# Dense per-head attention in a streaming two-layer decoder trunk

## The reference, cut to what matters

```
proj  = h @ w_in                       # 2048 query columns, 48 gate columns
q     = rms_norm(proj[:, :2048] per head of 128, q_gain)
gates = sigmoid(proj[:, 2048:])        # 3 branches x 16 heads
for each query block of 128 rows, each head (4 heads share one k, v):
    for branch in (compressed: 15 keys, selected: 256, window: 256):
        s = q . k / sqrt(128) - slope(head) * distance      # causal mask
        o += gate(branch, head) * softmax(s) @ v
out = concat(o) @ w_o
```

## Time and profile before

| | |
|---|---|
| median of 3 runs | 2630.6 us (2624.01 to 2635.27) |
| profiled execution, its own time | 2624.72 us |
| its span, first to last instruction | 2622.9 us |
| PE busy | 2535.5 us, 97% |
| DVE, ACT, POOL busy | 2154.7, 1251.6, 378.1 us |
| last product of `kv` to first of `wo` | about 1522.9 to 1768.6 us |
| first score product | about 1670.7 us |

### The profile page before, as it was taken

How to read it: one execution, slowest core, us unless ns; L and a number is a source line. 1 busy time by engine, 2 the same in 40 slices (tenths; PEclk the granted TensorE clock), 3 DMA queues, 4 the chain that set the end, 5 groups by cost and what they waited for, 6 DMA issues and landing times.

```text
span 2622.9 us, 38552 instructions
## 1 busy us (share of the span) xinstructions
PE 2535.5 (97%) x14006; PEld 2183.9 (83%) x14006; DVE 2154.7 (82%) x2593; ACT 1251.6 (48%) x1654; POOL 378.1 (14%) x205
## 2 busy tenths in 40 slices
PE   6998999998999999999999999999899999999999
PEld 4876888887888888888887888788788888888887
DVE  7887998999999889988899877678989756765665
ACT  4435343544554355535544444573555435543553
POOL 0000110231120012001142300363112001200110
PEclk8999999999999999999999989999999999999999
DMA  9997688886878877787776877208677655555553
GB/s 373 375 355 271 256 335 330 324 328 247 303 281 303 325 274 286 303 337 291 285 257 245 323 266 293 113 1 304 251 281 276 234 180 191 182 186 191 179 176 145
DMA packets 94312, 685.49 MB, mean 261 GB/s; under 512 B 10465, under 2 KB 10465, under 8 KB 11233
## 3 DMA queue, kind: packets, MB, share of 16 engines
q1 hardware_dynamic: 93746, 681.27, 69.4%
q10 hardware_dynamic: 432, 2.38, 0.2%
HBM read 681.51 MB, written 2.10 MB: 261 GB/s over the span
## 4 chain that ended last, share of the span: by engine, by line
PE 79%; DVE 6%; DMA 2%; issue 2%; ACT 1%; POOL 0%; DVEq 0%; ACTq 0%; SPq 0%
PE banks L1487 48%; PE banks L1489 25%; DMA raw<-in_stream 2%; DVE raw L1100 2%; DVE w_lo L1084 2%; PE banks L777 1%; ACT w_hi L921 1%; PE banks L1476 1%; PE banks L741 1%; PE banks L763 1%; DVE scratch L851 1%; PE banks L780 1%; DVE temp L1168 0%; PE banks L1478 0%; PE banks L743 0%
## 5 line engine op out<-in xcount | busy, mean ns | idle before, releaser
L1487 PE MATMUL banks<-h_op,w_hi 128*128 128x512 f32 x3840 | 1359.0, 399 | 25.6 <-DVE h_op L1174 18.2
L1084 DVE TENSOR_TENSOR w_lo<-raw,w_hi 128x1024 fp32r<-128x1024 f32 x841 | 1092.2, 1321 | 338.4 <-ACT w_hi L921 335.5
L921 ACT ACTIVATE w_hi<-raw 128x1024 fp32r<-128x1024 f32 x841 | 875.0, 1055 | 992.5 <-PE banks L1489 570.2
L1489 PE MATMUL banks<-h_op,w_lo 128*128 128x256 f32 x3840 | 1082.9, 282 | 0.0
L1487 PEld LDWEIGHTS banks<-h_op,w_hi 128*128 128x128 f32 x3840 | 726.0, 189 | 203.0 <-issue 23.8
L1487 PE MATMUL banks<-act_op,w_hi 128*128 128x512 f32 x2176 | 764.3, 397 | 0.3 <-DVE w_lo L1084 0.3
L1489 PEld LDWEIGHTS banks<-h_op,w_lo 128*128 128x128 f32 x3840 | 731.8, 191 | 0.0
L1489 PE MATMUL banks<-act_op,w_lo 128*128 128x256 f32 x2176 | 610.8, 281 | 0.0
L1100 DVE CUSTOM_DVE_ANT_0 raw<-raw,c_all 128x2048 f32<-128x2048 f32 x224 | 553.4, 2486 | 17.0 <-ACT c_all L895 9.5
L1487 PEld LDWEIGHTS banks<-act_op,w_hi 128*128 128x128 f32 x2176 | 409.4, 188 | 98.2 <-DVE w_lo L1084 1.2
L1489 PEld LDWEIGHTS banks<-act_op,w_lo 128*128 128x128 f32 x2176 | 412.2, 189 | 0.0
(11 more groups left out here) (158 smaller groups left out, 1369.8 us busy)
## 6 DMA issues: line engine op xcount, KB each, us to landing
raw<-in_stream SPq DMA_DIRECT2D x645, 1024.0 KB, 5.5
x_res<-in_x SPq DMA_DIRECT2D x1, 2048.0 KB, 11.6
out_x<-x_res SPq DMA_DIRECT2D x4, 512.0 KB, 4.4
mix_area<-in_w_s ACTq DMA_DIRECT2D x1, 1024.0 KB, 9.8
mix_area<-in_b_s ACTq DMA_DIRECT2D x1, 1024.0 KB, 14.3
small<-in_small SPq DMA_DIRECT2D x1, 682.0 KB, 16.6
attn_area<-in_pos ACTq DMA_DIRECT2D x1, 273.0 KB, 5.6
c_all<-in_c SPq DMA_DIRECT2D x1, 8.0 KB
```

Source lines behind the costliest of these rows:

```text
L921: act.activation(w_hi[:, out, 0:n], raw[:, slot, half:half + n], ACT.Copy).then_inc(hi_ready, 1)
L1084: dve.tensor_tensor(w_lo[:, out, 0:n], raw[:, slot, half:half + n], w_hi[:, out, 0:n].bitcast(F32), ALU.subtract).then_inc(stream, 2 if ch ...
L1487: pe.matmul(banks[:, g + j, :], hi[:, k, P * j:P * (j + 1)], operand[:, kt, :], start=(kt == 0), stop=False, skip_group_check=True)
L1489: last = pe.matmul(banks[:, g + j, 0:T], lo[:, k, P * j:P * (j + 1)], operand[:, kt, 0:T], start=False, stop=(kt == last_kt), skip_group_c ...
```

## The change

Four things are changed, all in layer 1 ahead of `wo`.

1. The order of the phases is now `kv`, `cmp`, `gate`, `q` (all four chunks). `h_op` is made during `cmp`. The pieces are the same 35; the first query chunk has three modulation pieces and the others two.
2. A query chunk is summed in one bank region: hi by the high tokens, hi by the low tokens, lo by the high tokens, each 256 columns (three products, each with its weight load, in place of two). ACT alone copies it out and squares it.
3. The prologue is cut into hooks that all engines call at fixed subs of the query chunks. Queries are now normed in place: sums of squares by group of four heads, root and inverse, spread over the partitions by PE, one multiplication on DVE. The last group's hooks lie in the attention loop. POOL makes a distance-times-slope table for every head.
4. The attention loop has 16 steps, one for a head with both query blocks. Scores are one product of 256 and one of 512 columns; DVE adds the bias table and takes the minimum in one instruction for each of four parts, from PSUM. The compressed branch is done once for four heads. Transposes go to one set of banks (six for each head), and the value product is done once for a group of four heads, in eight products of 512 columns (`weigh`).

The core of the diff:

```
-            phases.append(("q", [Chunk("q", 0, "F3", ("q", 0))]))
-            phases.append(("cmp", [Chunk("cmp", 0, "P0", ("cmp", 0))]))
-            phases.append(("q1", [Chunk("q", 1 + i, "P3", ("q", 0)) for i in range(3)]))
+            phases.append(("cmp", [Chunk("cmp", 0, "F3", ("cmp", 0))]))
             phases.append(("gate", [Chunk("gate", 0, "G1", ("gate", 0))]))
+            phases.append(("q", [Chunk("q", i, "P2" if i else "P3", ("q", 0)) for i in range(4)]))
...
+PE_HOOKS = {("q", 0, 1): [("keys", None)], ("q", 0, 4): [("cmp_keys", None)], ("q", 0, 6): [("spread_keys", None)],
+            ("q", 1, 2): [("gates", None)]}
+SPLIT_HOOKS = {("q", 0, 4): [("keys", None)], ("q", 0, 7): [("cmp_keys", None)], ("q", 1, 1): [("spread_keys", None)],
+               ("q", 1, 5): [("gates", None)]}
+for g in range(3):
+    PE_HOOKS.setdefault(("q", g + 1, 3), []).append(("sums", g))
+    PE_HOOKS.setdefault(("q", g + 1, 6), []).append(("spread", g))
...
+        def attention_act(act):
+            for i in range(NH + 7):
+                if i < NH:
+                    n, g, r = i, i // GRP, i % GRP
+                    for k, (qb, b, part) in enumerate(parts(n)):
+                        act.wait_ge(scores_biased, 2 * n + qb + 1)
+                        last = act.activation(part, part, ACT.Exp, scale=-1.0, bias=stat(n, NEG, k, 1),
+                                              accum_out=stat(n, DEN, k, 1))
...
+                if 2 <= i < NH + 2:
+                    act.wait_ge(weights_turned, n + 1)
...     (copies turned_low; for r == 0 four copies of turned_cmp)
+                if i >= 6 and (i - 6) % GRP == 0 and (i - 6) // GRP < NKV:
+                    act.wait_ge(pv_done, g + 1)
...     (two copies of 512 columns to act_op, out_hi)
+        def biased(dve, n):
+            dve.wait_ge(qk_done, n + 1)
+            for k, (qb, b, part) in enumerate(parts(n)):
+                last = dve.tensor_tensor_reduce(
+                    part, banks[:, 2 * (n % 2) + qb, keys * b:keys * (b + 1)], table(g, r)[:, T - keys:T], -1.0, 3e38,
+                    ALU.add, ALU.min, stat(n, NEG, k, 1))
...
+        def attention_dve(dve):
+            for i in range(NH + 7):
+                if i < NH:
+                    biased(dve, i)
+                if 1 <= i < NH + 1:
+                    weighted(dve, i - 1)
+                if i == 2:
+                    prologue_dve(dve, "sums", 3)
+                if i == 5:
+                    prologue_dve(dve, "spread", 3)
+                if 2 <= i < NH + 2:
+                    dve.wait_ge(weights_turned, n + 1)
+                    dve.tensor_copy(probs_t[:, 2:6, r, :], turned_high...)
+                if i >= 6 and (i - 6) % GRP == 0 and (i - 6) // GRP < NKV:
...     (two subtractions of 512 columns after out_hi, then out_lo)
+        def build_tables(pool):
+            pool.wait_ge(cmp_done, 1)
+            for g in range(NKV):
+                for r in range(GRP):
+                    last = pool.tensor_scalar(table(g, r), pos, -slopes[GRP * g + r], None, ALU.mult)
...
+        def attention_pe(pe):
+            score(pe, 0)
+            for i in range(NH + 7):
+                if i + 1 < NH:
+                    score(pe, i + 1)
+                if i == 1:
+                    prologue_pe(pe, "sums", 3)
+                if i == 4:
+                    prologue_pe(pe, "spread", 3)
+                if i >= 6 and (i - 6) % GRP == 0 and (i - 6) // GRP < NKV:
+                    weigh(pe, (i - 6) // GRP)
+                if 2 <= i < NH + 2:
+                    pe.wait_ge(weights_scaled, n + 1)
+                    if n:
+                        pe.wait_ge(turned_read, n)
+                        pe.wait_ge(turned_low_read, n)
...     (six transposes, then weights_turned)
...
+                    elif one_sum(cur.first):
+                                pe.matmul(out, hi[:, k, P * j:P * (j + 1)], operand[:, kt, 0:T],
+                                pe.matmul(out, hi[:, k, P * j:P * (j + 1)], operand[:, kt, T:HILO], start=False,
+                                last = pe.matmul(out, lo[:, k, P * j:P * (j + 1)], operand[:, kt, 0:T], start=False,
```

More of the change, by code:

```diff
@@ L513, in group @@
             return 4 * (prev.static(lambda c: c.n["c"] % 2))
[L516 to L526, removed]
@@ new lines, in scores, with parts, stat, out_of @@
+        def scores(n):
+            return attn_area[:, 768 * (n % 4):768 * (n % 4) + 768]
+        def parts(n):
+            sc = scores(n)
+            return [(0, 0, sc[:, 0:128]), (0, 1, sc[:, 128:256]), (1, 0, sc[:, 256:512]), (1, 1, sc[:, 512:768])]
+        def stat(n, kind, i=0, m=4):
+            o = 6688 + 16 * kind + 4 * (n % 4) + i
+            return attn_area[:, o:o + m]
+        NEG, DEN, COF = 0, 1, 2
+        def out_of(qb):
+            return banks[:, 6 + qb, :].rearrange("p (r t) -> p r t", r=GRP)
@@ new lines, in prologue_act @@
+        def prologue_act(act, what, g):
+            if what == "sums":
+                act.wait_ge(q_sums, g + 1)
+                act.activation(r_q, banks[0:GRP, 6, 0:T], ACT.Sqrt, scale=1.0 / HD, bias=eps[0:GRP, :]) \
+                    .then_inc(q_roots, 1)
+            if what == "keys":
+                act.wait_ge(vcmp_zeroed, 1)
+                act.wait_ge(cmp_done, 1)
+                for r in range(GRP):
+                    last = act.activation(vcmp[32 * r:32 * r + NCMP, :], banks[32 * r:32 * r + NCMP, 6, :], ACT.Copy)
+                act.activation(sq_c, banks[:, 5, 0:NB], ACT.Square).then_inc(cmp_keys_squared, 1)
+                act.wait_ge(square_sums, 1)
+                act.activation(r_k, banks[0:16, 7, 0:T], ACT.Sqrt, scale=1.0 / HD, bias=eps[0:16, :])                     .then_inc(rms_taken, 1)
+            if what == "cmp_keys":
+                act.wait_ge(square_sums, 2)
+                act.activation(r_c, banks[:, 5, 0:NB], ACT.Sqrt, scale=1.0 / HD, bias=eps[:, :]).then_inc(rms_taken, 1)
+            if what == "spread_keys":
+                act.wait_ge(zsum, BY_NAME["gate"][0].n["zsum"] + 1)
+                act.activation(gates_t, gates_t, ACT.Sigmoid).then_inc(gates_ready, 1)
@@ L1034, in evacuate @@
                     act.activation(vstat[:, 18:20], vstat[:, 20:22], ACT.Sqrt).then_inc(vrstd, 1)
-                if e == 3 and first and name == "wo":
+                if e == 0 and first and name == "wo":
+                    prologue_act(act, "sums", 3)
                     attention_act(act)
@@ L1051, in step @@
                                 evacuate_v(*what)
+                        for what in SPLIT_HOOKS.get((name, cur.first.loc, u), []) if name in ("q", "wo") else []:
+                            prologue_act(act, *what)
                         u += 1
@@ L1255, in step @@
                                 add_v(*what)
+                        for what in SPLIT_HOOKS.get((name, cur.first.loc, u), []) if name in ("q", "wo") else []:
+                            prologue_dve(dve, *what)
                         u += 1
@@ L1494, in step @@
                     last.then_inc(sub_done, 1)
+                    for what in PE_HOOKS.get((name, cur.first.loc, u), []) if name in ("q", "wo") else []:
+                        prologue_pe(pe, *what)
                     u += 1
@@ L1601, in position_table @@
     out = np.zeros((P, N_POS), np.float32)
+    d = P + np.arange(P)[:, None] - np.arange(T)[None, :]
+    out[:, 0:T] = np.where(d >= 0, d, BIG)
     for qb in range(2):
```

602 lines of the change are left out of this document (339 added, 263 removed).

## The result

| | before | after |
|---|---|---|
| median of 5 runs each | 2630.4 us (2624.0 to 2635.3) | 2647.8 us (2641.3 to 2649.5) |
| profiled execution, its span | 2622.9 us | 2639.5 us |
| last `kv` product to first `wo` product | 246.0 us | 265.9 us |

What follows compares the result with a forecast made beforehand. PE was taken to bound the kernel (busy 97% of the span). Terms 28.0 (compress) + 10.8 (gates, gap) + 116.9 (queries) + 119 (loop) = 274.7 against 245.7, 29 us longer: forecast 2657 us, range 2628 to 2692.

Steps and rivals of the forecast that it cites:

- The side and the mechanism: Attention loop: slower, as DVE's next steps queue behind the 6.8 us value block; `weigh` to `weigh` 22.7 us.
- The clock term: Attention loop: half clock between `weigh`s and cold starts add 15 us, giving 119; 3 to 5 of it in the filling.
- the full-clock chain: Attention loop: filling, intervals of 22.7, 22.7 and 22.2 us, then 6.8, together 104 us at full clock.
- The filling: Loop start: first exponential waits for last query sums, root and table load; first `weigh` at 29.7 us, clock 3 to 5 more.
- Compress weights: Compress weights run under the making of h, ending at 1550.9: 28.0 us of the changed stretch.
- Gates and gap: Between compress weights and first query product: gate products, then PE idle for 3 us; 10.8 us in all.
- Queries: Four query chunks: 92.2 us of products, 22.7 of PE hooks, 2 for the cold start; 116.9 us.
- Rival 4: Query chunks: weight load and product run one after the other, 84 us more, 2740 us; chance 0.04.
- Rival 3: DVE: dearer bias parts, tables holding up splits, more cold clock; +50 to +60 us, 2685; chance 0.12.
- The 26 us that these weights took by themselves are hidden: the main gain of the change: Compress weights: running them under the making of h hides the 26 us they took alone.
- Of the rivals, 2: Attention loop: same chain at full clock, 104 us for 119; 2641 to 2645 us in all; chance 0.16.
- Rival 1: Attention loop: PE bounds it, intervals 16.4 us, loop about 78; 2613 us with further savings; chance 0.10.

Runs made afterwards that it cites:

- the repeat: Second profiled execution of each kernel, before and after the change, with no edit: 2636.2 us (before) and 2648.6 us (after).
- the spare products: Changed kernel plus six unused 128-column PE products ahead of the turns of two heads in each group, filling PE's gaps: 2646.2 us, one run.
- all repairs: Changed kernel with compressed sum ahead of modulation pieces, output read early in halves, last query root after two heads' exponentials: 2633.5 us, ratio 1.0002 to before.

## Why the prediction was right, and where it was off

**The side and the mechanism held.** The prediction said slower, because PE and DVE would take turns around a block of value products, and the trace shows that chain wait by wait. Its steps from the start of `weigh`: copy of the turned weights from 8.5 us (measured 7.9), end of the two subtractions at 12.2 (11.6), next `weigh` at 22.7 at full clock (22.0 at clock 1.00). The experiment without the value products settles that the block is in series and not hidden. The size didn't hold: 29 us more were forecast, and the profiles and the runs give 10 to 20, 15 in the middle. In the stretch of after, 274.7 us forecast and 265.9 and 262.9 measured, the difference lies in the loop; the other terms were right to 1 us.

**The clock term was mis-sized.** "I take 15, so 119" was the step that failed. Measured are 109.8 and 106.1 us, where the full-clock chain alone had been put at 104. The step had two errors. First, it took the low clock of three microseconds (0.64) for every gap; the first interval of the repeat ran at 1.00 throughout. Second, it charged a slower PE to every interval, even where PE then waited for POOL or DVE anyway; with the spare products the intervals stayed at 22. What the clock did cost shows where PE's products stand on the chain: in the last value products (9.5 and 8.5 us, against 6.6 warm), where PE is the only engine at work, and once ahead of a `weigh` (the interval of 23.84 us). In all it is 6.1 us in the one profile and 2.4 in the other, against the loop of 103.7 with the spare products; the 15 also held 3 to 5 us for the filling. With the other waits repaired it is worth more: 94.8 against 89.6 us. (The Trainium skill, "TensorE: Matmul & The Clock Gate", Part 4, has the full clock not engage for transposes. By that rule, as the prediction used it, the loop would have been at 123 us, and it wasn't. A whole interval with 26 transposes in it ran at 1.00; but scores and value products stand between them, so this shows that they didn't bring the clock down, and not that they help to hold it up.)

**The filling was costed right for a wrong reason.** I had 29.7 us plus 3 to 5 for the clock; it took 31.6 and 32.2. But I took ACT's wait for the root as a given. It cost 7 us, more than any other single wait taken out here. It was a matter of where one call stands in ACT's order, and its lower clock went with it.

**The parts ahead of the loop held.** Compress weights, forecast 28.0 to the gates: 28.5 and 28.4. Gates and gap, 10.8: 9.9 and 10.7. Queries, 116.9 with hooks: 117.7 both times. Three products of 256 columns at 0.36 us: four chunks of 64 are 92.2, and the hooks are the rest. Their groups on PE are busy for 22.7 us in all, the forecast's number. That the sum fits so well is partly luck: the second compressed product (L832) took 2.4 us for 3.9, and the sums and spreads 1.4 more than their terms. The largest of them:

```profile
L821 PE MATMUL banks<-rstd,ident 4*128 4x256 f32 x24 | 6.0, 387 | 0.0
L815 PE MATMUL banks<-mix_area,pick 128*4 128x256 f32 x24 | 5.7, 379 | 0.0
...
L850 PE MATMUL banks<-mix_area,ident 16*128 16x256 f32 x16 | 4.1, 409 | 0.0
...
L839 PE MATMUL banks<-mix_area,pick 128*16 128x256 f32 x16 | 3.6, 380 | 0.0
```

Rival 4, weight loads that bound the queries, is out. Rival 3, more on DVE, too: the bias parts took 0.28 and 0.42 us, against the 0.29 and 0.43 that the line through the earlier trace rows gave.

**"The 26 us that these weights took by themselves are hidden: the main gain of the change" misread the sum.** The sum itself was right, since it counted four query chunks in the open. But the cover of the making of `h_op` was in use before, by query chunk 0, and the order alone changed nothing that can be told.

**Of the rivals, 2 came nearest.** It had the same chain at full clock, 2641 to 2645; the measured 2647.8 lies between it and the forecast. Rival 1, the loop bound by PE, would have needed intervals of 16.4 us; with all repairs and the spare products they were 20.2, 20.1 and 18.3 (the last without new scores), and even without most of the value products PE waited.

**What the pairs of profiles leave open.** The terms give 15 us in the mean of two pairs. The runs give 11 to 18, and 14 to 15 against the later runs of before. Two profiles of one kernel differ by 3 to 7 us in this stretch, so the terms can't be placed more finely.

## What to carry to other kernels

The same work in fewer, longer blocks with one set of banks can leave every engine less to do and still take longer, so follow one group through all engines in the order of their queues, and compare that interval, not the busiest engine's work, with the old one. When work moves under a cover, ask who had the cover, and cost what comes out. A lower clock in a stretch with waits is first of all a sign of the waits: price it only on products that stand on the chain, and take the wait out first.

## What the runs showed of the hardware

**Dense products at one of two paces.** With PE busy without a gap and clock 1.00, the same products ran at one of two paces, 2% apart, for hundreds of microseconds. The two windows, 400 to 480 and 2300 to 2380, for before and then for after (columns: length, PE busy with its count of products, clock, DMA):

```profile
400.00:480.00 80.00, 80.00 (x463) 1.00 0.85 324
2300.00:2380.00 80.00, 80.00 (x455) 1.00 0.52 188
```
```profile
400.00:480.00 80.00, 80.00 (x455) 1.00 0.83 317
2300.00:2380.00 80.00, 80.00 (x463) 1.00 0.55 195
```

The repeat of before had 464 and 454, the repeat of after 455 and 454, in code that is the same in all four. So the pace belongs to the execution and not to the kernel. With it, `kv` ended 9.6 us later in the profile of after, ahead of the first changed instruction, and 12.9 us came back behind the stretch. That is why the comparisons here are made by landmarks within the stretch and, where there are any, by medians of many runs. The landmarks in the stretch needn't be free of it: the same 386 products of three query chunks took 68.6 us in before and 70.7 in its repeat, at clock 0.97 and 0.96. What sets the pace is open.

**POOL beside DVE.** Each of POOL's tables of 256 columns had been costed at 1.12 us. The first eight took twice that, the second eight 1.0:

```profile
L793 POOL TENSOR_SCALAR mix_area<-scratch 128x256 f32<-128x256 f32 x8 | 17.2, 2156 | 30.2 <-PE banks L832 29.8
L793 POOL TENSOR_SCALAR temp<-scratch 128x256 f32<-128x256 f32 x8 | 8.0, 1006 | 0.5
```

DVE's splits beside the first eight took 1.15 to 1.17 us each, as long as without POOL; those beside the second eight 1.37 and 1.25. So if the two got in each other's way, POOL lost most of the time and DVE little, and as nobody waited for the tables then, it cost nothing that shows: PE was busy throughout. (The Trainium skill, "SBUF — State Buffer", "Who interferes with whom", has the one that issues first hold the shared ports and the other wait. I had weighed 8 us more for DVE by it; no such loss is seen. Whether the rule explains POOL's doubled time, no run here tells: the two groups of tables also differ in where they are written.)
